# First norm of a streaming encoder step, moved into the arrival of the input tiles, one Trainium2 core

## The chip, the cores and the metric

The program runs on one core of a Trainium2 chip. The metric is the device time of one execution in microseconds (us); for the kernel before it is 3312.23 us, the median of three runs.

## The reference, cut to what matters

The reference is a two-layer encoder step over 1152 tokens (1024 of a prompt and 8 x 16 of running streams) of width 1024, in float32. The part that matters here is the beginning of layer 0:

```python
def _rmsnorm(x, g):
    y = x32 * lax.rsqrt(jnp.mean(x32 * x32, axis=-1, keepdims=True) + EPS) * g
h = _rmsnorm(x, norm_g[0, 0])
p = h @ w_in                 # 8 gates, 512 q, 512 k, 1024 v, 1024 o
...
x = x + _rmsnorm(mixer(p), norm_g[0, 1])
```

So the kernel needs two things of x: the normalised activations, as the input of the first linear layer, and the plain x for the residual sum. All the rest (matrix memory, two feed-forward blocks, differential attention) follows and is computed in the same way by both kernels.

## The kernel before, in words

Activations lie feature-major in SBUF: 8 blocks (KT) of 128 features, each with 1152 tokens, so a token tile of 128 rows has to be turned by TensorE before it is used. Every linear layer is done in float32 accuracy with two float32r parts: activations XHI and XLO, weights WHI and WLO, and three products hi*hi, lo*hi, hi*lo. A *unit* is 128 output features: 8 blocks x 3 products x 3 token groups of 384 columns, 72 matmuls. Its result, a *group*, fills three PSUM banks: banks 0 to 2 for an even group, 3 to 5 for an odd one. Banks 6 and 7 serve for turns.

Weights of a unit arrive by a DMA of SP into WRAW (two buffers), and GpSimd splits them in two instructions (`split`, L1598 to L1605, instructions at L1602 and L1604) once the unit two before has let its buffers go. That is the semaphore `unit_free`, which TensorE raises with the first matmul of the next unit. SP's list in order: constants CST, the gains GROW, the tables OH and RB, the gate bias BG (nine DMAs, all counted in `s_const`), the gate weights (L1532, L1533), the bias table once VectorE has copied it (`table_sp`, L947 to L949), and then the weights of unit after unit (`load`, L1524 to L1528).

The stage around the change, before the first unit:

- ScalarE issues the loads of three input tiles XL (L2006, 128 tokens x 1024), squares and sums each tile as it lands (L2012) into a column of RT, copies blocks 0 to 3 of the turned tile from PSUM to F0 (L2015) and issues the load of tile i+3.
- TensorE waits for all constants (L1834), turns the gains and multiplies the bias table (L1835, L1836), and turns the nine tiles (L1847), 8 transposes each, into banks 2(i%4) and 2(i%4)+1. VectorE copies blocks 4 to 7 of each turned tile (L2222).
- When all nine are in F0, ScalarE stores F0 to HBM (L2021, 4.6 MB, for the residual), and takes Ln and Exp of RT (L2023, L2025). TensorE spreads the root over all partitions (L1855), and ScalarE copies it to RS (L2027).
- `norm_split` (L2112 to L2120): for each block VectorE computes F0 * gain * RS (L2116), ScalarE rounds it to XHI (L2032), VectorE subtracts to XLO (L2110).
- `first_two` (called at L1859) computes units 0 (gates) and 1 (first of q) block by block, in step with that, unit 1 three blocks behind. Unit 2 begins with `linear("q_m", begun=1)` (L1860).

## Time and profile before

| | |
|---|---|
| runs | 3322.31, 3311.97, 3312.23 us; median 3312.23 |
| profiled execution, its own time | 3314.61 us |
| its span in the profile | 3312.7 us |
| mean granted clock of TensorE | 0.961 |
| TensorE busy | 3094.8 us, 93% of the span |
| VectorE / ScalarE / GpSimd busy | 38% / 21% / 29% |

The profile is of one execution. Its own time stands 2.4 us above the median of the three runs, its span 1.9 us below its own time. Times inside the profile are counted from the start of the span. A matmul row shows the time from issue to the modelled end, so neighbours overlap; the step from one start to the next is what a matmul costs in a stream.

### The profile page before, as it was taken

The numbers are of one execution on the slowest core, as the hardware profiler recorded it, in microseconds if no ns is written. First come the engines' busy times: TensorE is split into PE (matmuls) and PEld (weight loads), VectorE is DVE, ScalarE is ACT, GpSimd is POOL, SyncE is SP. The second block draws the span as 40 slices with busy tenths as digits, with TensorE's granted clock in tenths as the row PEclk, the third lists the DMA queues.
The fourth block names the chain that finished last, engine by engine and source line by source line (L and its number), as shares of the span: only waits on it lengthen the run. The fifth ranks groups of instructions, "written<-read, shape, count | busy, mean of one in ns | idle before, by whom it ended". The sixth has DMA issues, their size and how long they took to land.

```text
span 3312.7 us, 45400 instructions
## 1 busy us (share of the span) xinstructions
PE 3094.8 (93%) x18477; PEld 2933.6 (89%) x18477; DVE 1244.5 (38%) x1551; ACT 708.6 (21%) x1212; POOL 951.1 (29%) x509
## 2 busy tenths in 40 slices
PE   6999988889999999998899978878989999999998
PEld 6999877879999999998799955656969999999998
DVE  4100254343333333334431047855253333333335
ACT  4111343241000000002210047744140000000003
POOL 2333100323333333333232322110433333333331
PEclk8999887999999999999999979999989999999999
DMA  4122301301111111111212321037211111111111
GB/s 156 39 80 60 96 29 36 114 26 45 39 43 44 38 44 40 42 44 38 78 47 83 92 79 39 14 114 256 96 30 40 45 38 44 41 41 44 38 45 64
DMA packets 237697, 200.92 MB, mean 61 GB/s; under 512 B 8545, under 2 KB 202494, under 8 KB 237074
## 3 DMA queue, kind: packets, MB, share of 16 engines
q1 hardware_dynamic: 194402, 147.93, 14.3%
q10 hardware_dynamic: 43184, 51.46, 4.6%
q8 instruction: 76, 1.25, 0.2%
q14 instruction: 35, 0.29, 0.0%
HBM read 166.30 MB, written 33.06 MB: 60 GB/s over the span
## 4 chain that ended last, share of the span: by engine, by line
PE 84%; DVE 7%; ACT 3%; issue 3%; ACTq 1%; DMA 1%; DVEq 1%; POOL 0%; POOLq 0%; SPq 0%
PE PS L1664 24%; PE PS L1668 24%; PE PS L1670 24%; PE PS L1101 1%; DVE XLO L2125 1%; DVE P L1321 1%; PE PS L1055 1%; PE PS L1135 1%; DVE F L2132 1%; PE PS L523 1%; PE PS L1760 1%; DVE F L2136 1%; PE PS L500 1%; PE PS L1085 1%; ACT P L1210 1%
## 5 line engine op out<-in xcount | busy, mean ns | idle before, releaser
L1664 PE MATMUL PS<-XHI,WHI 128*128 128x384 f32 x3672 | 850.0, 339 | 77.5 <-DVE XLO L2125 44.7
L1602 POOL TENSOR_TENSOR WHI<-WRAW,ZERO 128x1024 fp32r<-128x1024 f32 x197 | 373.5, 1896 | 1792.5 <-PE PS L1664 1738.2
L1668 PE MATMUL PS<-XLO,WHI 128*128 128x384 f32 x3672 | 841.0, 337 | 0.0
L1670 PE MATMUL PS<-XHI,WLO 128*128 128x384 f32 x3672 | 840.5, 336 | 0.0
L1664 PEld LDWEIGHTS PS<-XHI,WHI 128*128 128x128 f32 x3672 | 655.9, 190 | 98.9 <-issue 64.3
L1668 PEld LDWEIGHTS PS<-XLO,WHI 128*128 128x128 f32 x3672 | 661.1, 189 | 0.0
L1670 PEld LDWEIGHTS PS<-XHI,WLO 128*128 128x128 f32 x3672 | 661.0, 190 | 0.0
L1604 POOL TENSOR_TENSOR WLO<-WRAW,WHI 128x1024 fp32r<-128x1024 f32 x197 | 489.7, 2486 | 30.4 <-issue 6.9
L2203 DVE TENSOR_TENSOR F<-F,PS 128x1152 f32<-128x1152 f32 x176 | 238.2, 1354 | 278.3 <-PE PS L1670 278.3
L1988 ACT ACTIVATE HHI<-HF 128x1152 fp32r<-128x1152 f32 x44 | 51.4, 1169 | 990.4 <-DVEq L2184 990.4
L1664 PE MATMUL PS<-HHI,WHI 128*128 128x384 f32 x1056 | 244.2, 339 | 5.3 <-DVE HLO L2186 5.3
L1668 PE MATMUL PS<-HLO,WHI 128*128 128x384 f32 x1056 | 244.1, 339 | 0.0
L1670 PE MATMUL PS<-HHI,WLO 128*128 128x384 f32 x1056 | 243.9, 339 | 0.0
L2183 DVE TENSOR_TENSOR HF<-PS,SG 128x1152 f32<-128x1152 f32 x44 | 59.7, 1357 | 367.8 <-PE PS L1670 367.4
L1664 PEld LDWEIGHTS PS<-HHI,WHI 128*128 128x128 f32 x1056 | 190.6, 189 | 6.3 <-DVE HLO L2186 5.9
L1670 PEld LDWEIGHTS PS<-HHI,WLO 128*128 128x128 f32 x1056 | 191.4, 189 | 0.0
L1668 PEld LDWEIGHTS PS<-HLO,WHI 128*128 128x128 f32 x1056 | 190.8, 189 | 0.0
L2171 DVE TENSOR_TENSOR SG<-PS,RS 128x1152 f32<-128x1152 f32 x44 | 59.7, 1358 | 301.9 <-PE PS L1670 278.5
L2186 DVE TENSOR_TENSOR HLO<-HF,HHI 128x1152 fp32r<-128x1152 f32 x44 | 138.3, 3144 | 56.4 <-ACT HHI L1988 56.4
L1983 ACT ACTIVATE SG<-SG 128x1152 f32<-128x1152 f32 x44 | 51.4, 1168 | 472.5 <-DVEq L2172 472.2
L2177 DVE TENSOR_TENSOR SG<-SG,RS 128x1152 f32<-128x1152 f32 x44 | 103.3, 2348 | 31.3 <-ACTq L1984 31.3
L1321 DVE CUSTOM_DVE_ANT_0 P<-PS,BROW 128x128 f32<-128x128 f32 (+7 forms) x128 | 96.7, 755 | 27.0 <-PE PS L1055 14.2
(301 smaller groups left out, 2456.6 us busy)
## 6 DMA issues: line engine op xcount, KB each, us to landing
WRAW<-in_ffn_w_in_dram SPq DMA_DIRECT2D x88, 512.0 KB, 3.8
WRAW<-in_ffn_w_out_dram SPq DMA_DIRECT2D x44, 512.0 KB, 3.6
KC<-in_cache_k_dram SPq DMA_DIRECT2D x16, 1024.0 KB, 10.4
VC<-in_cache_v_dram SPq DMA_DIRECT2D x16, 1024.0 KB, 6.9
WRAW<-in_mlstm_w_in_dram SPq DMA_DIRECT2D x24, 512.0 KB, 3.9
xs_scratch<-F ACTq DMA_DIRECT2D x2, 4608.0 KB, 12.7
F<-xs_scratch ACTq DMA_DIRECT2D x2, 4608.0 KB, 13.9
WRAW<-in_kv_w_dram SPq DMA_DIRECT2D x16, 512.0 KB, 3.9
```

What stands on the lines that cost most here:

```text
L1321: dve.tensor_tensor_reduce(probs(n, j)[:, 0:w], sflat(n, j, w), BROW[n % 2][:, SEQ - w:], -1.0, 3e38, ALU.add, ALU.min, stat(n, 4 + j))
L1602: pool.tensor_tensor(WHI[par][:, :, :], WRAW[par][:, :, :], bc(bc(ZERO[:, 0], KT), P), ALU.add)
L1604: pool.tensor_tensor(WLO[par][:, :, :], WRAW[par][:, :, :], WHI[par][:, :, :].bitcast(F32), ALU.subtract).then_inc(w_split, 1)
L1664: mm = pe.matmul(out[:, c, :], wh, rhs_hi[:, chunk(c)], start=first, stop=False)
L1668: pe.matmul(out[:, c, :], wh, rhs_lo[:, chunk(c)], start=False, stop=False)
L1670: mm = pe.matmul(out[:, c, :], wl, rhs_hi[:, chunk(c)], start=False, stop=last)
L1983: act.activation(SG[:, :, :], SG[:, :, :], ACT.Silu)
L2171: dve.tensor_tensor(SG[:, :, :], G(o), rs, ALU.mult).then_inc(group_free[o % 2], 1)
L2177: dve.tensor_tensor(SG[:, :, :], SG[:, :, :], RS[:, :].rearrange("p (c t) -> p c t", c=NC), ALU.mult)
L2183: dve.tensor_tensor(HF[:, :, :], G(o), SG[:, :, :], ALU.mult).then_inc(group_free[o % 2], 1)
L2186: dve.tensor_tensor(HLO[:, t, :].rearrange("p (c t) -> p c t", c=NC), HF[:, :, :], HHI[:, t, :].rearrange("p (c t) -> p c t", c=NC).bitcas ...
L2203: dve.tensor_tensor(f, f, G(o), ALU.add).then_inc(group_free[o % 2], 1)
```

## The change

The norm is computed token-major, on each input tile as it lands, where the root is a scalar of the partition. The gain of the first norm is loaded into a tile GX, repeated on all 128 partitions (a DMA of 512 KB, second in SP's list). ScalarE squares tile i+1 ahead of its copies for tile i; GpSimd scales the sum and takes the power -0.5; VectorE multiplies tile, root and gain to XNN. TensorE turns both the plain tile (for F0; both halves through bank 5) and XNN (banks 6 and 7), 16 transposes a tile. ScalarE copies the turned XNN to XHI and VectorE subtracts to XLO, both straight from PSUM. As soon as three tiles are split, TensorE computes one token group of 384 columns of units 0 and 1 (`unit_chunk`, 24 matmuls) between the turns. GpSimd's splits of the weights of units 0 and 1 stand among the roots. The group `norm_in`, `norm_split`, RS of the first norm and the Ln and Exp of RT are gone; all groups move down by one, so that each takes the other set of banks. The store of F0 follows the last tile as before.

The diff, cut to its core:

```diff
-CONSTS = 9 * 16
+CONSTS = 8 * 16
+        XNN = [r(f"XNN{i}", [P, D]) for i in range(2)]
+        SQJ = at("SQJ", base + FB + 4 * 4096, [P, D])
+        GX = at("GX", base + FB + 5 * 4096, [P, D])
@@ sync
-            const(CST[:, :], consts)
+            sp.dma_start(CST[:, :], consts).then_inc(cst_landed, 16)
+            sp.dma_start(GX[:, :], bass.AP(norm_g.tensor, norm_g.offset, [[0, P], [1, D]])).then_inc(gx_landed, 16)
@@ gpsimd
-            pool.memset(HALF[:, :], -0.5).then_inc(unit_free, 1)
+            pool.memset(HALF[:, :], -0.5).then_inc(unit_free, 2)
-            split(0, 0, 32)
-            run(U0["q_m"], 24)
+            for i in range(NT):
+                pool.wait_ge(x_sq, i + 1)
+                pool.tensor_scalar(RT[:, i:i + 1], RT[:, i:i + 1], 1.0 / D, EPS, ALU.mult, ALU.add)
+                pool.drain()
+                pool.tensor_tensor(RT[:, i:i + 1], RT[:, i:i + 1], HALF[:, 0:1], ALU.pow).then_inc(x_rstd, 1)
+                if i == 1:
+                    split(0, 0, 32)
+                if i == 4:
+                    single(U0["q_m"])
+            single(U0["q_m"] + 1)
+            run(U0["q_m"] + 2, 22)
@@ tensor
+            def raw_half(i, half):
+                if half:
+                    pe.wait_ge(xt_act, i + 1)
+                elif i:
+                    pe.wait_ge(xt_dve, i)
+                for k in range(4):
+                    mm = pe.transpose(PS[:, 5, k * P:(k + 1) * P], XL[i % 3][:, (4 * half + k) * P:(4 * half + k + 1) * P], ident)
+                mm.then_inc(raw_tr, 1)
+            def turn_tile(i):
+                pe.wait_ge(xl_landed[i % 3], 16 * (i // 3 + 1))
+                raw_half(i, 0)
+                pe.wait_ge(xnn_ready, i + 1)
+                for half in range(2):
+                    if i:
+                        pe.wait_ge(nrm_lo, 2 * i - 1 + half)
+                    for k in range(4):
+                        mm = pe.transpose(PS[:, 6 + half, k * P:(k + 1) * P],
+                                          XNN[i % 2][:, (4 * half + k) * P:(4 * half + k + 1) * P], ident)
+                    mm.then_inc(nrm_tr, 1)
+                raw_half(i, 1)
+            def unit_chunk(u, c):
+                o = G0["gates"] + u
+                pe.wait_ge(w_split, u + 3)
+                if c == 0:
+                    free_wait(o, 0, 0)
+                if u and c == NC - 1:
+                    pe.wait_ge(xt_dve, NT)
+                pe.wait_ge(nrm_lo, 6 * (c + 1))
+                for k in range(KT):
+                    wh, wl = WHI[u][:, k, :], WLO[u][:, k, :]
+                    mm = pe.matmul(G(o)[:, c, :], wh, XHI[:, k, chunk(c)], start=k == 0, stop=False)
+                    if u and c == NC - 1 and k == 0:
+                        mm.then_inc(unit_free, 1)
+                    pe.matmul(G(o)[:, c, :], wh, XLO[:, k, chunk(c)], start=False, stop=False)
+                    mm = pe.matmul(G(o)[:, c, :], wl, XHI[:, k, chunk(c)], start=False, stop=k == KT - 1)
+                if c == NC - 1:
+                    mm.then_inc(group_ready, 1)
+            pe.wait_ge(cst_landed, 16)
+            turn_tile(0)
             pe.wait_ge(s_const, CONSTS)
-            (the nine tiles, the spread of the root, first_two)
+            pe.transpose(PS[:, 0, 0:81], GROW[:, :], CST[0:81, C_ID:C_ID + 81]).then_inc(g_ready, 1)
+            pe.matmul(PS[0:DH, 1, 0:TBL], RB[:, :], OH[:, :], start=True, stop=True).then_inc(tb_mm, 1)
+            for i in range(1, 4):
+                turn_tile(i)
+            pe.wait_ge(g_copied, 1)
+            pe.wait_ge(tb_cp, 1)
+            unit_chunk(0, 0)
+            turn_tile(4)
+            unit_chunk(1, 0)
+            turn_tile(5)
+            turn_tile(6)
+            unit_chunk(0, 1)
+            turn_tile(7)
+            unit_chunk(1, 1)
+            turn_tile(8)
+            unit_chunk(0, 2)
+            unit_chunk(1, 2)
             linear("q_m", begun=1)
@@ scalar
+            def square_x(i):
+                act.wait_ge(xl_landed[i % 3], 16 * (i // 3 + 1))
+                act.activation(SQJ[:, :], XL[i % 3][:, :], ACT.Square, accum_out=RT[:, i:i + 1])
+                act.drain().then_inc(x_sq, 1)
+            square_x(0)
             for i in range(NT):
+                if i + 1 < NT:
+                    square_x(i + 1)
+                act.wait_ge(raw_tr, 2 * i + 1)
+                act.activation(F0[:, 0:4, tile(i)], PS[:, 5, :]..., ACT.Copy).then_inc(xt_act, 1)
+                for half in range(2):
+                    act.wait_ge(nrm_tr, 2 * i + 1 + half)
+                    act.activation(XHI[:, 4 * half:4 * half + 4, tile(i)], PS[:, 6 + half, :]..., ACT.Copy).then_inc(nrm_hi, 1)
                 if i + 3 < NT:
+                    act.wait_ge(raw_tr, 2 * i + 2)
                     load_x(i + 3)
             act.dma_start(XS, F0[:, :, :]).then_inc(x_saved, 16)
-            (Ln and Exp of RT, the copy to RS, the eight copies to XHI)
@@ vector
+            def normed_x(i):
+                dve.wait_ge(x_rstd, i + 1)
+                if i >= 2:
+                    dve.wait_ge(nrm_tr, 2 * i - 2)
+                dve.scalar_tensor_tensor(XNN[i % 2][:, :], XL[i % 3][:, :], RT[:, i:i + 1], GX[:, :], ALU.mult, ALU.mult
+                                         ).then_inc(xnn_ready, 1)
+            dve.wait_ge(gx_landed, 16)
+            normed_x(0)
             for i in range(NT):
+                if i + 1 < NT:
+                    normed_x(i + 1)
+                dve.wait_ge(raw_tr, 2 * i + 2)
+                dve.tensor_copy(F0[:, 4:8, tile(i)], PS[:, 5, :]...).then_inc(xt_dve, 1)
+                for half in range(2):
+                    dve.wait_ge(nrm_hi, 2 * i + 1 + half)
+                    ks = slice(4 * half, 4 * half + 4)
+                    dve.tensor_tensor(XLO[:, ks, tile(i)], PS[:, 6 + half, :]...,
+                                      XHI[:, ks, tile(i)].bitcast(F32), ALU.subtract).then_inc(nrm_lo, 1)
+                if i == 1:
+                    (the copies of GALL and TBS, now from banks 0 and 1)
-            (the nine copies to F0, norm_split)
```

## Rows read from the trace of the kernel before

**Rows 1.** The page: spans and the chain that ended last.

```profile
PE 3094.8 (93%) x18477; PEld 2933.6 (89%) x18477; DVE 1244.5 (38%) x1551; ACT 708.6 (21%) x1212; POOL 951.1 (29%) x509
PE 84%; DVE 7%; ACT 3%; issue 3%; ACTq 1%; DMA 1%; DVEq 1%; POOL 0%; POOLq 0%; SPq 0%
```

**Rows 2.** Stretches (length, busy by engine, PEclk, DMA, GB/s); last, sum of 73:371.

```profile
40.00:60.00 20.00, 14.30 (x72) 13.69 (x73) 19.35 (x15) 8.87 (x8) 0.00 (x0) 0.83 0.20 57
...
sum 298.00, PE 295.59 PEld 294.24 DVE 23.46 ACT 47.87 POOL 99.68; mean PE 98.53 PEld 98.08 DVE 7.82 ACT 15.96 POOL 33.23
```

**Rows 3.** TensorE's timeline: start, length, line, shapes, count, [idle before <- releaser].

```profile
11.78 4.96 PE L1847 MATMUL PS<-CST,XL 128*128 128x128 f32 x24
28.52 1.09 PE L1847 MATMUL PS<-CST,XL 128*128 128x128 f32 x8 [1.22 <-DMA XL<-in_x_sample_dram]
44.00 1.30 PE L1664 MATMUL PS<-XHI,WHI 128*128 128x384 f32 x3 [5.72 <-DVE XLO L2110]
45.09 1.16 PE L1668 MATMUL PS<-XLO,WHI 128*128 128x384 f32 x3
46.97 0.69 PE L1664 MATMUL PS<-XHI,WHI 128*128 128x384 f32 x3
47.49 0.68 PE L1668 MATMUL PS<-XLO,WHI 128*128 128x384 f32 x3
72.85 0.80 PE L1664 MATMUL PS<-XHI,WHI 128*128 128x384 f32 x3
```

**Rows 4.** ScalarE's timeline.

```profile
6.70 1.06 ACT L2012 ACTIVATE XN<-XL 128x1024 f32<-128x1024 f32 x1 [3.25 <-DMA XL<-in_x_prompt_dram]
7.66 0.19 ACT L2012 ACTIVATION_READ_ACCUMULATOR XN<-XL 128x1 f32 x1
15.49 0.60 ACT L2015 ACTIVATE F<-PS 128x512 f32<-128x512 f32 x1
```

**Rows 5.** VectorE's timeline.

```profile
11.89 0.55 DVE L2219 COPY TBS<-PS 8x384 f32<-8x384 f32 x1 [1.13 <-PE PS L1836]
15.49 0.69 DVE L2222 COPY F<-PS 128x512 f32<-128x512 f32 x1 [1.01 <-PE PS L1847]
43.94 1.42 DVE L2116 SCALAR_TENSOR_TENSOR XN<-F,GALL,RS 128x1152 f32<-128x1152 f32 x1
45.28 1.35 DVE L2110 TENSOR_TENSOR XLO<-XN,XHI 128x1152 fp32r<-128x1152 f32 x1
66.60 1.41 DVE L2235 TENSOR_SCALAR IG<-PS,BG 4x1152 f32<-4x1152 f32 x1 [3.36 <-PE PS L1670]
```

**Rows 6.** GpSimd's small operations, by shape: busy, mean ns, idle before.

```profile
L1015 POOL TENSOR_TENSOR RSTD<-MSQ,HALF 128x8 f32<-128x8 f32 x8 | 13.1, 1639 | 1.2
L450 POOL TENSOR_TENSOR DEN<-DEN,HALF 128x4 f32<-128x4 f32 x9 | 9.1, 1010 | 186.7 <-ACT DEN L646 186.7
L1013 POOL TENSOR_SCALAR MSQ<-SSQ 128x8 f32<-128x8 f32 x8 | 1.6, 196 | 41.0 <-ACTq L1234 41.0
```

**Rows 7.** GpSimd's timeline, the splits.

```profile
10.49 1.89 POOL L1602 TENSOR_TENSOR WHI<-WRAW,ZERO 128x1024 fp32r<-128x1024 f32 x1 [8.51 <-DMA WRAW<-in_mlstm_w_in_dram]
68.38 1.89 POOL L1602 TENSOR_TENSOR WHI<-WRAW,ZERO 128x1024 fp32r<-128x1024 f32 x1 [29.05 <-PE PS L1664]
70.41 2.39 POOL L1604 TENSOR_TENSOR WLO<-WRAW,WHI 128x1024 fp32r<-128x1024 f32 x1
75.42 3.33 POOL L1604 TENSOR_TENSOR WLO<-WRAW,WHI 128x1024 fp32r<-128x1024 f32 x1
```

**Rows 8.** Stretches again, of the tiles' arrival.

```profile
6.00:8.00 2.00, 0.00 (x0) 0.00 (x0) 0.00 (x0) 1.15 (x2) 0.00 (x0) 1.00 1.04 395
22.54:25.81 3.27, 3.27 (x16) 2.81 (x16) 1.22 (x2) 3.17 (x6) 0.00 (x0) 0.57 0.79 234
```

**Rows 9.** DMA issues of the first 80 us: count, KB each, us to landing.

```profile
XL<-in_x_prompt_dram ACTq DMA_DIRECT2D x8, 512.0 KB, 5.5
WRAW<-in_mlstm_w_in_dram SPq DMA_DIRECT2D x5, 512.0 KB, 3.9
```

More of the change, by code:

```diff
@@ L106 @@
          "q_a": 8, "k_a": 8, "v_a": 8, "out_a": 8, "ffn1": 6 * FG}
-GROUPS = {"norm_in": 1, "gates": 1, "q_m": 4, "k_m": 4, "v_m": 8, "o_m": 8, "out_m": 8,
+GROUPS = {"gates": 1, "q_m": 4, "k_m": 4, "v_m": 8, "o_m": 8, "out_m": 8,
           "post0": 1, "ffn0": 12 * FG, "post1": 1, "q_a": 8, "k_a": 8, "v_a": 8,
@@ L1831, in ffn @@
                 group(FG - 1, True)
-            pe.wait_ge(s_const, CONSTS)
-            pe.transpose(PS[:, 7, 0:81], GROW[:, :], CST[0:81, C_ID:C_ID + 81]).then_inc(g_ready, 1)
-            pe.matmul(PS[0:DH, 6, 0:TBL], RB[:, :], OH[:, :], start=True, stop=True).then_inc(tb_mm, 1)
-            for i in range(NT):
-                pe.wait_ge(xl_landed[i % 3], 16 * (i // 3 + 1))
-                if i == 3:
-                    pe.wait_ge(g_copied, 1)
-                    pe.wait_ge(tb_cp, 1)
-                if i >= 4:
-                    pe.wait_ge(xt_act, i - 3)
-                    pe.wait_ge(xt_dve, i - 3)
-                for k in range(KT):
-                    b = 2 * (i % 4) + k // 4
-                    mm = pe.transpose(PS[:, b, (k % 4) * P:(k % 4 + 1) * P], XL[i % 3][:, k * P:(k + 1) * P], ident)
-                mm.then_inc(xt_ready, 1)
@@ L1849, in _ @@
-            pe.wait_ge(xt_act, NT)
-            pe.wait_ge(xt_dve, NT)
-            free_wait(G0["norm_in"], 0, 0)
-            pe.wait_ge(rt_ready, 1)
-            for t in range(NT):
-                mm = pe.matmul(G(G0["norm_in"])[:, t // 3, (t % 3) * P:(t % 3 + 1) * P], bc(RT[:, t], P), ident, start=True, stop=True)
-                if t == 0:
-                    mm.then_inc(unit_free, 1)
-            mm.then_inc(group_ready, 1)
-            first_two(0, G0["gates"], 0)
+            def raw_half(i, half):
[6 more added lines that the diff above has]
+                mm.then_inc(raw_tr, 1)
@@ L2022, in _ @@
             act.wait_ge(w_split, 2)
-            act.activation(RT[:, :], RT[:, :], ACT.Ln, bias=EPSC[:, 0:1], scale=1.0 / D)
-            act.drain()
-            act.activation(RT[:, :], RT[:, :], ACT.Exp, scale=-0.5).then_inc(rt_ready, 1)
-            act.wait_ge(group_ready, G0["norm_in"] + 1)
-            act.activation(RS[:, :].rearrange("p (c t) -> p c t", c=NC), G(G0["norm_in"]), ACT.Copy
-                           ).then_inc(group_free[G0["norm_in"] % 2], 1)
-            act.drain().then_inc(rs_ready, 1)
-            for k in range(KT):
-                act.wait_ge(xn_ready, k + 1)
-                act.activation(XHI[:, k, :], XN[k % 2][:, :], ACT.Copy).then_inc(x_hi, 1)
             act.wait_ge(x_split, KT)
@@ L2110, in low @@
                 dve.tensor_tensor(XLO[:, k, :], src, XHI[:, k, :].bitcast(F32), ALU.subtract).then_inc(x_split, 1)
-            def norm_split(n, gain):
-                for k in range(KT):
-                    dve.drain()
-                    dve.scalar_tensor_tensor(XN[k % 2][:, :], F0[:, k, :], gain(k), RS[:, :], ALU.mult,
-                                             ALU.mult).then_inc(xn_ready, 1)
-                    if k:
-                        low(n, k - 1, XN[(k - 1) % 2][:, :])
-                low(n, KT - 1, XN[(KT - 1) % 2][:, :])
             def low_gain(n, k, gain):
```

40 lines of the change are left out of this document (21 added, 19 removed).

## The prediction

> **What bounds the kernel now.** The page's chain comes first: TensorE holds 84% of it and is busy for 93% of the span [rows 1], so time is gained only where TensorE waits or does work that can go. The stretches show where this is. From 73 to 371 us it is busy for 295.6 of 298 us, so whatever moves the third unit, which starts at 72.85, moves everything behind it one to one [rows 2, 3]. I read the change as one question: when does the third unit start? Before that, TensorE does two units and waits. A triple of matmuls steps on by 0.52 us (46.97 to 47.49) [rows 3], so two units of 24 triples are 25 us. They start only at 44.00, behind the last tile (turned at 28.52), the roots, their spread and the first normalised block. Up to there some 32 us hold little but 72 transposes, and between 40 and 60 us TensorE is busy for 14.3 of 20 us, with a granted clock of 0.83 [rows 2, 3].
>
> **The change, part by part.** It cannot shorten the 25 us of units 0 and 1; it puts them among the tiles. Removed are the Ln, Exp, spread and copy of the root, and eight blocks of VectorE, ScalarE, VectorE in turn. Added are 72 more transposes, nine GpSimd roots, one 512 KB DMA. I work out the schedule in three pieces, then sum it.
>
> *Costs of one tile.* The last eight transposes at full clock took 1.09 us, about 0.107 each plus a tail; the first 24, after 10 us of rest, 4.96 us or 0.207 each, twice as long [rows 3]. Sixteen are 1.7 us warm, 3.3 cold (at the lower of the two clock levels, 1.2 GHz), plus 0.3 of handoffs. ScalarE: square and accumulator read 1.25, three copies of 0.60 [rows 4], about 3.0. VectorE: L2116 took 1.42 for 1152 columns, so 1.3 for 1024; copy 0.69; two subtractions of 512 columns as the copy, some 0.6 to 0.69 each [rows 5]: 3.2. GpSimd: 0.20 for the scaling and, from 1.01 at four columns and 1.64 at eight, about 0.54 for a power of one [rows 6]; with handoffs 0.95. No trace shows a one-column power: at most it is the four columns' 1.01, at least 0.38 (the part that doesn't grow), and I take 0.54. The engines nearly balance. The loop that sets the step runs over two tiles: turned half (0.7), copy to XHI (0.65), square of a later tile (1.35), root (0.95), XNN (1.3), then VectorE's copy and subtractions (1.9): 6.85, or 3.4 us a tile.
>
> *Up to the first chunk.* The first square starts at 6.70 [rows 4], its root is there at 8.9, but XNN waits for GX. At 6 to 8 us the DMA engines are full at 395 GB/s [rows 8], so 0.52 MB more push what lies behind it out by 1.3 us; I put GX at 10 us (bounds 9, if it takes turns with XL, and 12, if it queues behind all). XNN is ready at 11.3, TensorE has finished tile 0 at 14.0 (cold), VectorE at 15.9. GpSimd splits the gates' weights between the roots of tiles 1 and 2: these landed at 10.49 [rows 7], now about 11.7, plus 1.89 + 2.39 and handoffs is 16.2, the root of tile 2 is at 17.2 and its XNN at 18.5. Behind it stand 1.9 us for tile 1 (20.4) and the copies of gains and table, 0.8 [rows 5], so 21.3. Tile 2 then takes 1.3 + 1.9: 24.5. TensorE turns the last halves of tile 3 behind it, 1.7 cold: the first chunk starts at 26.0. The loads of tiles 3 and 4 (5.5 us [rows 9], issued at about 14 and 17.5) arrive before they are wanted.
>
> *Chunks and tiles 4 to 8.* A chunk is 24 matmuls of 0.173: 4.17 us. Five of them 20.85. The sixth ends with a wait: unit 2's weights are split only once the chunk's first matmul is through (0.34), then 1.89 + 2.39 and handoffs of 0.2 [rows 7], so 4.85 in place of 4.17. Before, this signal came three steps before the end and the split fitted (it ended at 72.80, the unit began at 72.85). The clock: from 44.00 to 46.97 three triples took 2.97 us where three at 0.52 take 1.56, a loss of 1.4 us [rows 3]; I charge the same once. Tiles 4, 5, 7 and 8 stand next to chunks, in whose shade ScalarE and VectorE finish: 2.0 each, 8.0. Tile 6 follows tile 5 directly and waits for its subtractions: 2.9. After tile 8 the third chunk of unit 0 waits for VectorE's copy and two subtractions: 2.0. Sum: 26.0 + 20.85 + 4.85 + 1.4 + 8.0 + 2.9 + 2.0 = 66.0. Against 72.85 that is **6.8 us less**.
>
> *Costed at nothing, with their cover.* Unit 1's weights are now loaded only after VectorE's table copy (21.3), because SP's list waits for that before `load`: issue at 22.0, landing at about 26.5 [rows 9], split by 31; the fourth root stands before that split, the fifth behind it (32), while the chunk that needs the weights starts at 33.6 and TensorE's tile 5 at 37.8. Were the cover of some 2.5 us gone, tiles would stall by what is missing. The store of F0 (4.6 MB) now runs from about 57 to 70 us, beside weight loads that have 8 us of room each. ScalarE gets a table load for the gates' Exp; nobody on TensorE's path waits for it. Banks changing sides cost nothing, since every group waits by the same rule.
>
> One row speaks of GpSimd's neighbour: the split at 75.42 took 3.33 in place of 2.39 us, beside VectorE work on two SBUF operands; the split at 68.38 beside VectorE's reading of PSUM at 66.60 kept its 1.89 [rows 5, 7]. On the path lies only the split that runs beside such a PSUM read, so I add nothing; in the tiles it could add 0.9 to a split, within the cover above. The Trainium skill says why ("GPSIMD Engine Reference", "Specifications": GpSimd's SBUF interfaces are shared with VectorE when that reads two SBUF operands); by this rule the two early splits, beside XNN's two SBUF operands, would each be late by up to 0.9, and only the first would show in the sum, as 66.9. The trace agrees for one split of the four shown.
>
> **The rivals.**
> 1. *The tiles flow better than I think* (chance 0.13). GX lands with tile 0 (-1.3), the gates' split finds a hole (-1.4), the array is warm at the first chunk (-1.4), tile 6 is hidden (-0.9), and the cold turn of tile 3 is warm (-0.8). The third unit at 60.2, 12.6 us gained: 3299.6. For it: the tiles arrive early enough. Against: it needs all of them.
> 2. *The clock takes the gain back* (0.17). While the tiles came one at a time, the granted clock fell to 0.57 between 22.5 and 25.8 us [rows 8]. At that level a triple steps by 0.99 (2.97 / 3 [rows 3]) in place of 0.52, so a chunk costs 3.8 us more. Two such chunks make 73.6, the third unit where it was: 3313.
> 3. *The clock makes it slower* (0.04). The same mechanism for the whole stage: the pauses around the tiles hold TensorE at the lower level throughout, and all six chunks run at 1.2 GHz: 6 x 3.8 - 1.4 and 5 tiles x 1.6 are 29 us more: third unit at 95, 3334.6. It decides from four and a half slow chunks on (16.8 us more than my sum). Against: a chunk is 4 us of dense matmuls, and at 44.00 it took less than 3 us of such to bring the clock back, even with waits of 0.8 and more behind. The Trainium skill has this as a rule against short bursts ("TensorE: Matmul & The Clock Gate", "HAM oscillation — how this bites in real kernels": the array that waits between bursts falls back to half clock and pays again at every burst). By that rule the time would be this rival's; the trace bears it out for the lone tiles only.
> 4. *The gain is eaten later* (0.06). Something behind 72.85 is not tied to TensorE, and the end stays at 3312. Against: 295.6 busy of 298 us [rows 2].
>
> **How the numbers follow.** My forecast has 0.60. It is a change in one stage, 6.8 us from the span of 3312.7, with the execution's own time 3314.6 going to 3307.8. The metric is the median of the runs shown, 3312.2, 2.4 below that execution, so 3305.4. A measurement of this kernel tells about 0.3% from no change, 9.9 us; the runs alone spread over 10. More than that is gained in rival 1 and in a corner of the forecast (0.16 together); lost in rival 3 and, by a little, where runs like the one of 3322 come to be the median (0.05). The range takes the bounds of GX and the root (one us either way), the clock charged not at all or twice, most of rival 1, and rivals 2 and 4: 3299 to 3315.
>
> **What would show it.** In the profile after, the first matmul triple at L1664's place of the third unit at 64 to 68 us, the first chunk at 25 to 27; GpSimd's third split ending within 0.1 us of it; gaps of some 2 us before tile 6's last halves and before the third chunk; a power of one column near 0.54; VectorE busy for about 3.2 us a tile. I am wrong if the first chunk begins past 30, if chunks step by 8 us, or if the third unit comes early and the span doesn't follow.

## The result, and the profile after

Over twelve runs each the changed kernel takes 3309.95 us (median, 3305.23 to 3312.13) and the kernel before 3315.34 (3311.97 to 3322.31): a ratio of 0.9983, with a 95% interval from 0.9975 to 0.9991. It is a gain of 5.4 us, within the 0.3% that the prediction called no change. Timed once more, among the experiments below, it had 3309.74 against 3316.77, ratio 0.9979 (0.9970 to 0.9988).

The profiled execution has a span of 3308.5 us, 4.2 less than before, and its own time was 3310.28. The page first, spans and chain [rows 1]:

```profile
PE 3101.3 (94%) x18531; PEld 2939.7 (89%) x18531; DVE 1243.5 (38%) x1562; ACT 704.7 (21%) x1217; POOL 957.3 (29%) x527
PE 86%; DVE 7%; ACT 3%; issue 2%; ACTq 1%; DVEq 1%; POOL 0%; DMA 0%; POOLq 0%
```

TensorE is busy for 6.5 us more than before, with 72 transposes added, and issue and DMA are a smaller part of the chain. TensorE's timeline of the stage (start, length, line, shapes, count, idle before), against [rows 3]:

```profile
10.88 1.97 PE L1870 MATMUL PS<-CST,XNN 128*128 128x128 f32 x8 [3.09 <-DVE XNN L2266]
12.64 1.06 PE L1859 MATMUL PS<-CST,XL 128*128 128x128 f32 x4
...
20.48 0.63 PE L1859 MATMUL PS<-CST,XL 128*128 128x128 f32 x4 [1.75 <-DVE F L2275]
...
24.15 1.09 PE L1859 MATMUL PS<-CST,XL 128*128 128x128 f32 x4 [0.88 <-DVE F L2275]
...
27.45 0.67 PE L1886 MATMUL PS<-XHI,WHI 128*128 128x384 f32 x1
...
32.29 0.60 PE L1859 MATMUL PS<-CST,XL 128*128 128x128 f32 x4
...
33.99 0.42 PE L1886 MATMUL PS<-XHI,WHI 128*128 128x384 f32 x1
...
41.09 0.63 PE L1859 MATMUL PS<-CST,XL 128*128 128x128 f32 x4 [0.88 <-DVE F L2275]
...
43.04 0.42 PE L1886 MATMUL PS<-XHI,WHI 128*128 128x384 f32 x1
...
57.28 0.41 PE L1886 MATMUL PS<-XHI,WHI 128*128 128x384 f32 x1 [2.07 <-DVE XLO L2279]
...
61.52 0.33 PE L1886 MATMUL PS<-XHI,WHI 128*128 128x384 f32 x1
...
66.48 0.79 PE L1683 MATMUL PS<-XHI,WHI 128*128 128x384 f32 x3 [0.63 <-POOL WLO L1614]
```

L1859 and L1870 are the turns, L1886 opens a chunk, L1683 the third unit. The chunks begin at 27.45, 33.99, 43.04, 48.99, 57.28 and 61.52, and the third unit at 66.48, where it was 72.85: **6.4 us earlier**. Three waits of TensorE are left behind the first chunk: 0.88 before tile 6, 2.07 behind tile 8, 0.63 before the third unit.

VectorE's timeline and then GpSimd's, in the same columns, show what sets the step of the first tiles [rows 5 to 7]:

```profile
9.54 1.28 DVE L2266 SCALAR_TENSOR_TENSOR XNN<-XL,RT,GX 128x1024 f32<-128x1024 f32 x1 [9.54 <-DMA GX<-in_norm_g_dram]
11.90 1.28 DVE L2266 SCALAR_TENSOR_TENSOR XNN<-XL,RT,GX 128x1024 f32<-128x1024 f32 x1 [1.08 <-POOL RT L1635]
...
18.45 1.28 DVE L2266 SCALAR_TENSOR_TENSOR XNN<-XL,RT,GX 128x1024 f32<-128x1024 f32 x1 [2.83 <-POOL RT L1635]
```

```profile
12.08 2.86 POOL L1612 TENSOR_TENSOR WHI<-WRAW,ZERO 128x1024 fp32r<-128x1024 f32 x1 [0.21 <-DMA WRAW<-in_mlstm_w_in_dram]
...
17.86 0.55 POOL L1635 TENSOR_TENSOR RT<-RT,HALF 128x1 f32<-128x1 f32 x1
...
64.04 2.38 POOL L1614 TENSOR_TENSOR WLO<-WRAW,WHI 128x1024 fp32r<-128x1024 f32 x1
```

XNN of the first tile waits for the gain (9.54), that of tile 2 for its root, 2.83 us (18.45). The root stands behind the split, whose first half took 2.86 us in place of 1.89: it began 0.18 us behind VectorE's multiply for tile 1 (11.90). A power of one column takes 0.55 us. The third unit's split ends at 66.42, and the unit starts at 66.48.

From the third unit to the end of the span the changed kernel takes 2.1 us more than the kernel before (3242.0 against 3239.9), so that of the 6.4 us the span keeps 4.2. Most of the 2.1 is in one place, where TensorE has just turned the last values and goes on with the next unit; the kernel before was there at 270.90:

```profile
264.42 0.47 PE L1784 MATMUL PS<-CST,RS 128*128 128x128 f32 x1 [1.17 <-ACT NSV L2022]
264.55 1.31 PE L1683 MATMUL PS<-XHI,WHI 128*128 128x384 f32 x3
265.65 1.16 PE L1687 MATMUL PS<-XLO,WHI 128*128 128x384 f32 x3
```

```profile
270.90 0.76 PE L1664 MATMUL PS<-XHI,WHI 128*128 128x384 f32 x3
271.50 0.68 PE L1668 MATMUL PS<-XLO,WHI 128*128 128x384 f32 x3
```

The same two triples start 1.10 us apart after and 0.60 before. In the 20 us around this place the granted clock is 0.91, where the kernel before had 1.00. Neither kernel changes a line there. Whether this belongs to the change was the first question for the experiments.

### The profile page after: what moved, and what is told of

Same layout as the page of the kernel before. It is cut to its first block, busy times and chain, and to the rows that moved or that the text cites. A ratio compares the mean times of both kernels' runs of the same rounds, so it can differ in the third digit from the quotient of the medians.

```text
span 3308.5 us, 45597 instructions
## 1 busy us (share of the span) xinstructions
PE 3101.3 (94%) x18531; PEld 2939.7 (89%) x18531; DVE 1243.5 (38%) x1562; ACT 704.7 (21%) x1217; POOL 957.3 (29%) x527
## 3 DMA queue, kind: packets, MB, share of 16 engines
q8 instruction: 76, 1.25, 0.2%
## 4 chain that ended last, share of the span: by engine, by line
PE 86%; DVE 7%; ACT 3%; issue 2%; ACTq 1%; DVEq 1%; POOL 0%; DMA 0%; POOLq 0%
PE PS L1683 24%; PE PS L1687 24%; PE PS L1689 24%; PE PS L1110 1%; PE PS L1064 1%; DVE XLO L2171 1%; DVE P L1330 1%; PE PS L1144 1%; DVE F L2178 1%; PE PS L532 1%; PE PS L1779 1%; PE PS L1094 1%; DVE F L2182 1%; PE PS L509 1%; DVE XLO L2166 1%
## 5 line engine op out<-in xcount | busy, mean ns | idle before, releaser
L1683 PE MATMUL PS<-XHI,WHI 128*128 128x384 f32 x3624 | 839.5, 339 | 69.8 <-DVE XLO L2171 43.6
L1687 PE MATMUL PS<-XLO,WHI 128*128 128x384 f32 x3624 | 830.5, 337 | 0.0
L1689 PE MATMUL PS<-XHI,WLO 128*128 128x384 f32 x3624 | 829.4, 336 | 0.0
L1683 PEld LDWEIGHTS PS<-XHI,WHI 128*128 128x128 f32 x3624 | 647.7, 190 | 90.6 <-issue 61.0
L1687 PEld LDWEIGHTS PS<-XLO,WHI 128*128 128x128 f32 x3624 | 653.2, 190 | 0.0
L1689 PEld LDWEIGHTS PS<-XHI,WLO 128*128 128x128 f32 x3624 | 652.2, 189 | 0.0
L1683 PE MATMUL PS<-HHI,WHI 128*128 128x384 f32 x1056 | 244.4, 340 | 5.3 <-DVE HLO L2232 5.3
L1683 PEld LDWEIGHTS PS<-HHI,WHI 128*128 128x128 f32 x1056 | 190.7, 189 | 6.3 <-DVE HLO L2232 5.9
```

The source lines that it names most:

```text
L1683: mm = pe.matmul(out[:, c, :], wh, rhs_hi[:, chunk(c)], start=first, stop=False)
L1687: pe.matmul(out[:, c, :], wh, rhs_lo[:, chunk(c)], start=False, stop=False)
L1689: mm = pe.matmul(out[:, c, :], wl, rhs_hi[:, chunk(c)], start=False, stop=last)
```

## Experiments

Two theories about the gain. **Laid in:** the chunks fill waits of TensorE, and each term of the prediction's schedule is real. **Shorter norm:** the token-major norm alone brings it, and the interleaving adds little. And one rival about the end: the later clock loss is part of the change. The measure is the start of the third unit. Two profiles of one kernel gave it within 0.1 us (66.48 and 66.56 for the change, 61.77 and 61.78 for e3). The experiments have one execution each, except the timed ones, and a single time is too coarse for such differences: the runs of the kernel before spread over 10 us.

### All tiles first (e1), and without splits among them (e5)

```diff
-            unit_chunk(0, 0)
-            turn_tile(4)
-            unit_chunk(1, 0)
...
+            for i in range(4, NT):
+                turn_tile(i)
+            for c in range(NC):
+                unit_chunk(0, c)
+                unit_chunk(1, c)
```

> The changed kernel, but all nine tiles are turned before the six chunks. Theory (the gain is TensorE's work laid into the waits of the tiles): the tiles take 3.4 to 3.9 us each without chunks beside them, plus some 4 us where the fifth root stands behind unit 1's split, so the last tile is split at about 50 and six chunks of 4.2 follow: third unit at 75 to 79 us, later than the 72.85 of before, the span some 10 us above the changed kernel's 3308.5. Rival (the gain is the shorter norm, the interleaving adds little): third unit at 66 to 69.

e5 adds, on GpSimd and in SP's list:

```diff
-                if i == 1:
-                    split(0, 0, 32)
-                if i == 4:
-                    single(U0["q_m"])
+            split(0, 0, 32)
+            single(U0["q_m"])
@@ sync
+            sp.dma_start(WRAW[1][:, :, :], w_in[:, :, 0:P]).then_inc(w_landed[1], 16)
             table_sp(sp)
... (the later load of the same weights is taken out)
```

> All tiles before the chunks, as in e1, and GpSimd's two splits behind the nine roots, the weights of unit 1 loaded ahead of the bias table. Theory (two things stretch the tiles: TensorE's cold transposes and the splits): without the splits no root is late, tile 2 comes 1 to 2 us earlier and tile 5 2 us earlier, but the splits, 8.8 us, now start at about 41 and end at 50, so the chunks of unit 1 wait for them: third unit at 72 to 75, about where e1 has it. Rival (the splits cost little among the tiles): third unit after 76.

TensorE's timelines, e1 and then e5:

```profile
48.05 0.42 PE L1886 MATMUL PS<-XHI,WHI 128*128 128x384 f32 x1
...
73.90 0.79 PE L1683 MATMUL PS<-XHI,WHI 128*128 128x384 f32 x3 [0.63 <-POOL WLO L1614]
```

```profile
23.42 0.63 PE L1861 MATMUL PS<-CST,XL 128*128 128x128 f32 x4 [1.55 <-DVE F L2271]
...
26.49 0.63 PE L1861 MATMUL PS<-CST,XL 128*128 128x128 f32 x4 [0.88 <-DVE F L2271]
...
30.24 0.63 PE L1861 MATMUL PS<-CST,XL 128*128 128x128 f32 x4 [1.55 <-DVE F L2271]
...
43.44 0.42 PE L1888 MATMUL PS<-XHI,WHI 128*128 128x384 f32 x1
...
69.28 0.81 PE L1685 MATMUL PS<-XHI,WHI 128*128 128x384 f32 x3 [0.63 <-POOL WLO L1618]
```

Without interleaving the third unit starts at 73.90, a microsecond later than in the kernel before. So the order of the chunks brings 7.4 us, and as e1 ran, the token-major norm alone brought nothing. The expectation had 75 to 79; the split cost less than the 4 us that I gave it there. In e5 the third unit comes 4.6 us earlier (69.28). Up to tile 7 its tiles step by 3.75 and 3.07 us in turn (23.42 to 26.49 is 3.07, 26.49 to 30.24 is 3.75), 3.4 in the mean, the number that the prediction worked out.

The 4.6 us are not the splits' alone. Laid side by side, the tiles' steps of e1 are longer than those of e5 at two places where a root stands behind a split (0.75 us up to tile 2, 2.1 at tile 5) and at three more, before tiles 4, 6 and 7 (1.45, 0.9 and 0.8), where the granted clock was 0.50: eight transposes took up to 1.91 us there and 1.16 in e5. By this reckoning e1 lost about 2.9 us to the splits and 3.1 to the clock. Against that stand 1.4 us that e5 lost at tile 8: its gates' split began at 37.76, and VectorE's multiply for that tile, begun at 38.02, took 2.72 us in place of 1.28.

My expectation for e5 (72 to 75) was wrong: I let the splits start at 41 and hold up the chunks of unit 1. The gates' split ended at 42.96, before the first chunk (43.44), and that of unit 1 at 47.35, under this chunk, just before the chunk that needs it. The shorter norm is thus worth 3.6 us by itself in e5, with GpSimd free up to the last tile and the clock up; in e1 splits and clock took all of it.

### The gates' split moved (e2)

```diff
-                if i == 1:
+                if i == 3:
                     split(0, 0, 32)
```

> The changed kernel, with GpSimd's split of the gates' weights after the fourth root instead of the second. Theory: VectorE's wait of 2.83 us for the root of tile 2 falls to the square's time, the first chunk starts about 0.9 us earlier (26.5 in place of 27.45), and the third unit 0.9 earlier (65.6). Rival (TensorE's cold transposes set the step of the first tiles): nothing moves by more than 0.3.

VectorE, GpSimd and TensorE of e2:

```profile
16.22 1.28 DVE L2266 SCALAR_TENSOR_TENSOR XNN<-XL,RT,GX 128x1024 f32<-128x1024 f32 x1 [0.67 <-POOL RT L1635]
...
21.22 2.91 DVE L2266 SCALAR_TENSOR_TENSOR XNN<-XL,RT,GX 128x1024 f32<-128x1024 f32 x1
```

```profile
21.15 1.89 POOL L1612 TENSOR_TENSOR WHI<-WRAW,ZERO 128x1024 fp32r<-128x1024 f32 x1
23.19 3.15 POOL L1614 TENSOR_TENSOR WLO<-WRAW,WHI 128x1024 fp32r<-128x1024 f32 x1
```

```profile
24.87 0.80 PE L1859 MATMUL PS<-CST,XL 128*128 128x128 f32 x4 [3.17 <-DVE F L2275]
```

Tile 2's XNN starts at 16.22 in place of 18.45, as expected, and the third unit at 66.67, not one bit earlier. Neither side had foreseen why: VectorE's multiply of tile 3 began 0.07 us behind the split and took 2.91 us in place of 1.28, and the split's second half took 3.15 in place of 2.36. The gain at tile 2 went into TensorE's wait of 3.17 us before tile 3. The first chunk began at 27.91, not at the 26.5 that I expected.

### The chunks of unit 1 cut (e3)

The third argument is the range of k that a call works through. The last piece of the middle chunk, the one marked True, raises unit_free in place of the last chunk. (The lines in `unit_chunk` that take the range are left out here.)

```diff
             unit_chunk(0, 0)
             turn_tile(4)
-            unit_chunk(1, 0)
+            unit_chunk(1, 0, range(0, 4))
             turn_tile(5)
+            unit_chunk(1, 0, range(4, 8))
             turn_tile(6)
             unit_chunk(0, 1)
             turn_tile(7)
-            unit_chunk(1, 1)
+            unit_chunk(1, 1, range(0, 3))
             turn_tile(8)
+            unit_chunk(1, 1, range(3, 7))
             unit_chunk(0, 2)
+            unit_chunk(1, 1, range(7, 8), True)
             unit_chunk(1, 2)
```

> The changed kernel, with the chunks of unit 1 cut: half of the first one between tiles 4 and 5 and half between 5 and 6, three eighths of the second between 7 and 8, four eighths behind tile 8, one eighth behind the last chunk of unit 0, with the signal for the weights of unit 2. Theory: TensorE's waits of 1.3 us before tile 6, 2.07 behind tile 8 and 0.8 before the third unit go, since each has work in it now: third unit at 62.5 to 63. Rival (VectorE and ScalarE are at their limit there, or GpSimd's split): the waits turn up at other places, third unit not before 65.5.

TensorE's timeline of e3, and its waits up to 62.5 us (line waited for: us in total, times, longest):

```profile
26.73 0.42 PE L1886 MATMUL PS<-XHI,WHI 128*128 128x384 f32 x1
...
61.77 0.80 PE L1683 MATMUL PS<-XHI,WHI 128*128 128x384 f32 x3
```

```profile
...
PE PS L1870 <- DVE XNN L2269: 3.1, 1, 3.1
PE PS L1859 <- DVE F L2278: 2.6, 2, 1.7
```

The third unit starts at 61.77, 4.7 us before the change's and 0.7 below the range that I gave. The waits behind the first chunk are gone from the table and came up nowhere else. Of the 4.7, 0.7 are the first chunk's start (26.73 in place of 27.45) and 0.6 its clock (it takes 4.26 us, in the change 4.84); the rest, 3.4, stands against the 3.58 of the three waits (0.88, 2.07 and 0.63). This is the strongest evidence for "laid in": the same work, in an order that leaves no hole, is shorter by the time of the holes.

### The array kept busy (e4, e9)

```diff
+            def busy(n):
+                for _ in range(n):
+                    pe.matmul(PS[:, 7, 0:TC], bc(HALF[:, 0], P), bc(HALF[:, 0], TC), start=True, stop=True)
...
+            pe.wait_ge(unit_free, 2)
+            busy(5)
             pe.wait_ge(cst_landed, 16)
             turn_tile(0)
@@ turn_tile
                 raw_half(i, 0)
+                if i == 0:
+                    busy(4)
```

> The changed kernel, with nine idle matmuls on TensorE before the first tile's normalised half (results not used). Theory: the transposes of tiles 0 to 3 and the first chunk ran at the lower clock level; from here on they take half of it. Tile 0 ends 1.2 us earlier, the root of tile 2 (behind the split) absorbs that; the first chunk gains 0.7 and tile 3 0.8: third unit at 65 to 65.3. Rival (the clock falls again among the tiles, so that the first chunk starts slow as it does now): third unit at 66 to 66.5 as without.

e9 is e3 with this (in PSUM bank 2), and with `busy(6)` before tile 2 and `busy(1)` before tile 3.

> The kernel of e3, with idle matmuls not only before the first tile (e4: the clock fell again in the 4.35 us wait for tile 2's root) but also in the waits before tiles 2 and 3. Theory: the granted clock stays at the full level from 9 us on, tiles 0 to 3 take half of TensorE's time, the first chunk starts at 26.1 and runs at full speed; but VectorE and the root of tile 2 set the step, so little comes of it: third unit at 61.0 to 61.5, 0.3 to 0.7 before e3. Rival (the lower clock was what held the first tiles): 60 or earlier.

e4's stretches (length, busy of PE, PEld, DVE, ACT, POOL, granted clock, DMA), then TensorE of e9:

```profile
16.00:20.40 4.40, 0.05 (x1) 0.03 (x1) 2.03 (x3) 1.40 (x3) 3.94 (x5) 0.75 0.37 119
20.40:28.20 7.80, 6.92 (x32) 6.55 (x33) 6.01 (x9) 4.59 (x8) 1.91 (x4) 0.50 0.61 163
```

```profile
26.05 0.42 PE L1892 MATMUL PS<-XHI,WHI 128*128 128x384 f32 x1
...
32.97 0.45 PE L1892 MATMUL PS<-XHI,WHI 128*128 128x384 f32 x1 [0.72 <-POOL WLO L1614]
...
35.95 0.63 PE L1859 MATMUL PS<-CST,XL 128*128 128x128 f32 x4 [0.60 <-DVE F L2289]
```

In e4 the turns of tiles 0 and 1 ran at twice the speed, then TensorE stood for 4.35 us and the clock fell to 0.50 (1.2 GHz of 2.4); the first chunk started at 28.22 and the third unit at 66.78, 0.3 above the range of the rival and far from my 65 to 65.3. In e9 the clock stayed up and the first chunk started at 26.05, as expected. But the third unit came at 62.63, 0.9 after e3's, not before it. Now TensorE met the split of unit 1 (0.72 us) and its follower on VectorE (0.60). Two things came together there: TensorE was 0.7 us earlier, and the weights of unit 1 landed 1.5 us later than in e3 (28.53 against 27.04), though they were asked for at the same time (22.8). The cover that the prediction had counted as 2.5 us was thin already in the change, where this split ended at 32.48 and its chunk began at 33.99; in t1 the chunk waited 0.30 us for it. In e9 it was gone, and what was missing appeared as a wait, by the rule that the prediction gave.

### The gain's DMA (e6), the gates' weights first (e8)

e6 sets GX to 1.0 and loads nothing, so it leaves out the gain of the first norm. e8 is e3 with the gates' weights third in SP's list and their split behind the first root.

```diff
-            sp.dma_start(GX[:, :], bass.AP(norm_g.tensor, norm_g.offset, [[0, P], [1, D]])).then_inc(gx_landed, 16)
@@ gpsimd
+            pool.memset(GX[:, :], 1.0).then_inc(gx_landed, 16)
```

> The changed kernel without the 512 KB DMA of the gain; GX is set to 1.0, so the gain of the first norm is left out of the computation. Theory of the prediction (the DMA pushes what lies behind it out by 1.3 us): the first XNN starts at 8.8 in place of 9.54, the gates' weights land at 10.7 in place of 12.0, the root of tile 2 is 1.2 earlier, and the third unit at 65.3 in place of 66.48. Rival (hidden): XNN of tile 2 and the third unit where they were, within 0.3.

```diff
...
+            sp.wait_ge(s_zero, 1)
+            gv = w_in[:, :, 3072:3080]
+            sp.dma_start(WRAW[0][:, :, 0:MH], gv[:, :, 0:MH]).then_inc(w_landed[0], 16)
+            sp.dma_start(WRAW[0][:, :, 32:32 + MH], gv[:, :, MH:2 * MH]).then_inc(w_landed[0], 16)
@@ gpsimd
-                if i == 1:
+                if i == 0:
                     split(0, 0, 32)
```

> The kernel of e3, with the gates' weights third in SP's list and their split behind the first root. e2 showed a split beside XNN stretching VectorE's multiply from 1.28 to 2.91 us. Theory: the split now runs in 9 to 13.5, where VectorE has slack, tile 2's XNN starts at about 16.3 in place of 18.45, and the first chunk and the third unit come 0.9 to 1.5 us earlier than in e3: third unit at 60.3 to 60.9. Rival (it stretches the XNN of tiles 0 or 1 instead, or the many small packets hold up the input tiles): third unit at 61.8 or later.

TensorE and a stretch of e6, then GpSimd and VectorE of e8:

```profile
24.95 0.42 PE L1886 MATMUL PS<-XHI,WHI 128*128 128x384 f32 x1
...
65.47 0.81 PE L1683 MATMUL PS<-XHI,WHI 128*128 128x384 f32 x3 [0.63 <-POOL WLO L1614]
```

```profile
56.00:59.00 3.00, 3.00 (x11) 3.00 (x11) 0.03 (x2) 0.00 (x0) 0.00 (x0) 0.50 0.91 393
```

```profile
11.56 1.89 POOL L1613 TENSOR_TENSOR WHI<-WRAW,ZERO 128x1024 fp32r<-128x1024 f32 x1 [2.80 <-DMA WRAW<-in_mlstm_w_in_dram]
```

```profile
16.96 1.28 DVE L2270 SCALAR_TENSOR_TENSOR XNN<-XL,RT,GX 128x1024 f32<-128x1024 f32 x1 [6.28 <-POOL RT L1636]
```

Without the DMA the first XNN starts at 8.98 (9.54), the root of tile 2 is there 1.25 us earlier, and the third unit is at 65.47, near the 65.3 that I expected. The first chunk, at 24.95, is 2.5 us earlier than in the profile of the change, but there the clock was low at tile 3 and here it wasn't. Behind tile 8 it fell to 0.50 here, and the last two chunks took 1.6 us more. t1, the change once more (below), happens to have the clock of e6: up at tile 3, low in the last two chunks. Against it every chunk of e6 begins 1.1 us earlier, the first (26.02 to 24.95) as the third unit (66.56 to 65.47). That is the price of the DMA, near the 1.3 of the prediction. It holds although GpSimd's split and XNN of tile 1 met the other way round in e6, where VectorE paid.

e8 went wrong at its own place: third in the list, the weights landed at 11.56, only half a microsecond earlier than at its end (12.08 in the change), and the root of tile 1, now behind their split, kept VectorE waiting for 6.28 us. Third unit at 64.99. An in-order engine should not be given something that waits for a DMA ahead of something that is ready.

### The timed runs (t1, t2, e10)

t1 is the change again, t2 the kernel of e3. e10 is e9 with the load of unit 1's weights ahead of the bias table, as in e5.

> The changed kernel once more, timed beside the others. Theory (the third unit's start is fixed by the schedule, the rest varies with TensorE's clock): third unit at 66.3 to 66.7 again; what follows takes 3240 to 3247 us, whichever; the mean of the runs 5 to 7 us below before. Rival (the 2.2 us given back are part of the change): what follows takes 3242 within 0.5 again.

> The kernel of e3, timed. Theory: third unit at 61.8 to 62.5 (by the clock of the first chunk), 4 to 4.7 us before the change's, and the median of its runs 3 to 6 us below the change's, 9 to 12 below before. Rival (the clock gives such gains back later): within 2 us of the change.

> The kernel of e9 (chunks cut, idle matmuls in the first waits), with the weights of unit 1 asked for ahead of the bias table. In e9 the split of unit 1 ended at 32.9 and TensorE waited 0.72 us for it and 0.60 for the tile behind. Theory: the weights land before 20, the split follows the fifth root at 25.9 and ends by 31 (beside XNN, which it stretches while VectorE has slack), both waits go: third unit at 61.2 to 61.6, against 62.63 in e9. Rival (the split beside XNN holds up tile 4): 62.5 or later.

| kernel | third unit | runs: median (lowest to highest) | ratio to before |
|---|---|---|---|
| before | 72.85 | 3316.77 (3311.66 to 3322.26), 23 runs | |
| change, t1 | 66.56 | 3309.74 (3308.14 to 3312.24), 11 | 0.9979 (0.9970 to 0.9988) |
| chunks cut, t2 | 61.78 | 3307.54 (3303.55 to 3313.21), 12 | 0.9973 (0.9964 to 0.9981) |
| e10 | 60.51 | 3303.53 (3301.84 to 3304.44), 5 | 0.9959 (0.9946 to 0.9972) |

TensorE of t1, the first chunk and the third unit:

```profile
26.02 0.42 PE L1886 MATMUL PS<-XHI,WHI 128*128 128x384 f32 x1
...
66.56 0.79 PE L1683 MATMUL PS<-XHI,WHI 128*128 128x384 f32 x3 [0.63 <-POOL WLO L1614]
```

VectorE of e10, then the start of its third unit:

```profile
25.20 2.91 DVE L2284 SCALAR_TENSOR_TENSOR XNN<-XL,RT,GX 128x1024 f32<-128x1024 f32 x1 [0.16 <-POOL RT L1639]
```

```profile
60.51 0.79 PE L1687 MATMUL PS<-XHI,WHI 128*128 128x384 f32 x3
```

The first chunk of t1 begins 1.4 us before that of the change's first profile, and its third unit at the same time: with the clock up at tile 3 the first chunk came at 26.02, and with the clock low behind tile 8 the last two took 10.77 us in place of 9.20.

e10 is the best of all: each of its five runs is below every run of the change, and the median is 13.2 us below before. The split beside XNN stretched VectorE's multiply to 2.91 us again, but under the first chunk, where VectorE had the room. The third unit came at 60.51, earlier than my 61.2 to 61.6. t2 is 2.2 us below the change where its third unit is 4.8 earlier; the spread of its runs, 9.7 us, is wider than that difference, so it fits neither side well. Against the kernel before it is 9.2 us, at the lower end of my 9 to 12.

### Where the rest of the gain goes

Stretches of each profile, all behind the third unit: up to the first matmul of the memory stage (L461 in the kernel before, L470 in the changed one), from there to the first sum of the norm behind it, the feed-forward block (ffn), the stretch from the attention's start to the last sum of the norm behind it, and the rest:

| profile | third unit | to memory | memory | ffn | attention | rest | all behind third unit |
|---|---|---|---|---|---|---|---|
| before | 72.85 | 299.5 | 322.9 | 869.2 | 481.0 | 891.6 | 3239.9 |
| change | 66.48 | 301.0 | 323.3 | 869.3 | 481.4 | 891.4 | 3242.0 |
| t1 | 66.56 | 301.0 | 323.9 | 869.3 | 481.9 | 891.2 | 3243.0 |
| e1 | 73.90 | 299.5 | 324.0 | 869.2 | 480.3 | 891.9 | 3240.6 |
| e2 | 66.67 | 300.8 | 323.1 | 869.2 | 482.2 | 890.5 | 3241.5 |
| e3 | 61.77 | 299.5 | 324.2 | 869.2 | 483.3 | 892.0 | 3243.9 |
| t2 | 61.78 | 301.0 | 323.4 | 869.3 | 483.3 | 892.0 | 3244.6 |
| e4 | 66.78 | 299.5 | 327.6 | 869.3 | 481.1 | 891.3 | 3244.4 |
| e5 | 69.28 | 299.5 | 322.8 | 869.2 | 481.8 | 890.8 | 3239.8 |
| e6 | 65.47 | 299.5 | 328.9 | 869.3 | 481.0 | 891.9 | 3246.3 |
| e8 | 64.99 | 299.5 | 329.4 | 869.3 | 482.2 | 890.6 | 3246.7 |
| e9 | 62.63 | 301.0 | 323.3 | 869.3 | 481.2 | 891.3 | 3241.7 |
| e10 | 60.51 | 300.8 | 323.1 | 869.3 | 481.1 | 891.3 | 3241.2 |

(375.6 or 375.7 us lie between the feed-forward block and the attention in all of them.) Where TensorE is dense (ffn), the rows agree to 0.1 us. The stretch up to the memory stage has two values, 299.5 and 301, and the memory stage goes from 322.8 to 329.4. Two kernels with the third unit within 0.3 us of each other, the change and e4, have one value and the other; so does the same kernel twice, e3 and t2. The first 50 us of the memory stage in e5 and in e8:

```profile
368.80:418.80 50.00, 45.21 (x242) 40.61 (x243) 23.76 (x78) 20.22 (x55) 2.05 (x2) 0.80 0.43 127
```

```profile
364.50:414.50 50.00, 46.39 (x201) 40.97 (x201) 21.53 (x70) 18.88 (x51) 2.04 (x2) 0.62 0.44 127
```

The work is the same (45 and 46 us of TensorE), but the granted clock is 0.80 in one and 0.62 in the other. The expectation of t1 had 3240 to 3247 for what follows, a range that could hardly fail; it was 3243.0. Its rival, 3242.0 within 0.5, falls, if narrowly. Two profiles can't decide by so little, but the timed runs can, if the third unit starts in every run of a kernel where its profile has it. The median span less this start is 3242.1 us for the kernel before (23 runs), 3241.7 and 3241.3 for the change (12 and 11 runs) and 3241.2 for e10 (5 runs). For the first twelve runs of the kernel before, whose spans I don't have, the times give about 3240.7, if a span is 1.8 us below its time as in the others. So the change lies 0.4 to 0.8 us below the kernel before in one series and 1.0 above it in the other: what its first profile seemed to give back is in the main a difference between executions, of stages that it doesn't touch, and a loss of 1 us at most can't be told from none.

The cut kernel is the exception: 3243.9 (12 runs), and both its profiles, e3 and t2, have 483.3 us in the attention, more than all others. It fits this that t2 is only 2.2 us faster than the change. The cut alone is not the cause, since e9 and e10 have the same cut and 481.2 and 481.1 there; what is, stays open.

## Why the prediction was right

The forecast was the first case, a third unit at 66.0 and a gain below what this kernel's measurement tells from none; the third unit came at 66.48. The range, 3299 to 3315, holds the time, and the class, no change by 0.3%, is right. The mechanism held: the chunks fill waits (e1, e3), and what the third unit gains, the end gains (timed runs). Point by point (TensorE's timeline gives the steps):

| term | forecast | measured |
|---|---|---|
| first XNN starts | 10.0 | 9.54 |
| root of tile 2 | 17.2 | 18.4 |
| VectorE behind the copies of tables | 21.3 | 22.1 |
| first chunk starts | 26.0 | 27.45 |
| five chunks, with the clock's charge | 20.85 + 1.4 = 22.25 | 21.89 |
| tiles 4, 5, 7, 8 | 4 x 2.0 | 4 x 1.70 |
| tile 6 | 2.9 | 3.07 |
| behind tile 8 | 2.0 | 2.31 |
| last chunk and split | 4.85 | 4.96 |
| third unit | 66.0 | 66.48 |

- **The sum was partly lucky.** It is off by 0.5 us, but its terms are off by more: 1.45 too little up to the first chunk, 0.4 too much for the chunks and the clock, 1.2 too much for tiles 4, 5, 7 and 8, and 0.6 too little for the rest. The class would also have been right for a change that gains nothing; it is the start of the third unit that tests the forecast.
- **The first chunk, 1.45 late.** Two terms add up. I let the split of the gates' weights run in 4.4 us; it took 5.36, from 12.08 to 17.44, because VectorE multiplied XNN of tile 1 in the same time. I had priced just this (0.9, "only the first would show in the sum, as 66.9") and left it out of the sum; it should have been in. It made VectorE's end of tile 2 some 0.7 us late (25.2 for 24.5). The other half is the turn of tile 3: I had its last halves alone at the lower level (and 24.5 and 1.7 are 26.2, not 26.0), but its first half, too, began only at 24.15, behind VectorE's copy, so that all sixteen transposes took 3.3 us. In t1, with the split just as late (5.31 us) but the clock up, they took 1.96, and the first chunk began at 26.02: the forecast's number, by errors that cancel. The Trainium skill ("GPSIMD Engine Reference", "Specifications") says that the two engines share interfaces; the runs agree, and show that either of them can be the one that pays: in the change the split, in e2 VectorE, 1.63 us.
- **The clock.** I charged 1.4 on a chunk and 0.8 on the turn of tile 3. In the change's profile it cost 0.6 in the first chunk (4.84 us against 4.26 in e3) and 1.3 at tile 3. In t1, the same kernel, it cost nothing there (first chunk 4.24 us long) and 1.6 in the last two chunks, so that the third unit came at the same time. Rivals 2 and 3 were thus real as a mechanism, at a price of 1.6 to 2.0 and not 7.6 or more. The Trainium skill has a rule against short bursts ("TensorE: Matmul & The Clock Gate", "HAM oscillation — how this bites in real kernels"). It agrees with e4, where the clock went down to 0.50 around a wait of 4.35 us; in e3, with only short waits behind the first chunk, no chunk was stretched. Behind tile 8 the rows don't follow from the wait alone: it was 2.07 us in the change, e2, e4, e6 and t1, and the last two chunks were stretched in e6 and t1 only.
- **Costed at nothing.** The weights of unit 1 landed at 28.04, not 26.5, and their split ended at 32.48, not 31. The cover was 1.5 us in place of 2.5, still enough here; in t1 it was missing by 0.30 us, and in e9 by more.
- **The tiles beside chunks** took 1.70, not 2.0: sixteen warm transposes and hardly any handoff, since VectorE and ScalarE had finished under the chunk.
- **The power of one column**: taken as 0.54, measured 0.55.
- **The step of a tile**, 3.4 us: in e5, where no split disturbs the loop up to tile 7, 3.07 and 3.75 in turn.
- **Rival 1** (the tiles flow better): its parts exist, but not together. e2 found no hole for the split; t1 and e9 found the warm array worth 1.4 us at the first chunk; only cutting the chunks took tile 6's wait. e10 arrives at 60.51, near the 60.2 of this rival, but by another way: its array is warm and tile 6 is hidden, yet GX still lands at 9.44 and the root of tile 2 still waits for the split, and two waits that the rival left in place (behind tile 8, before the third unit) are gone.
- **The median.** 3305.4 was forecast, 3309.95 measured. Of the 4.6 us, 3.1 are the base: the three runs shown had a median of 3312.2, and twelve have 3315.3. Those three were too few for a figure of this size. The rest is the difference in the gain, 6.8 against 5.4. The third unit accounts for 0.5 of it; the remaining 0.9 is small beside the spread of the runs, 7 us for the change and 10 for the kernel before.
- **Rival 4** (eaten later) did not come true: over the timed runs the part behind the third unit takes the same time in both kernels, to about 1 us. What made it look so in one profile was TensorE's clock, by which this part differs from one execution to the next.

## What to carry to other kernels

Work laid into the waits of a ramp is worth those waits and no more, so list the waits that remain after it and cut the filling work to fit them; here pieces of half a chunk took out 3.4 us that whole chunks had left. Before judging a change of a few microseconds by times, find the point behind which nothing differs and compare when each kernel gets there, and compare profiles in which the clock fell at the same places (t1 and e6). In an in-order queue, put what waits for a DMA behind what is ready, and don't let GpSimd's big elementwise work meet VectorE's two-operand work, unless VectorE has the room.
